# Value rows of a routed expert mixer gathered and summed one step behind the dot products, with the weights formed behind the next routing

## What is computed

```
q      = normalised h @ w_pq                   # 8 heads, two halves each
i_top  = top 16 of 128 keys in each half
e      = top 16 of the 16 x 16 sums            # 16 experts of 16384, per token and head
act    = gelu(h . expert_u[e])                 # 16 dot products of 1024
out    = sum over heads and 16 experts of softmax(score) * act * expert_v[e]
y      = layer_norm(alpha * h + out)
```

## Time and profile before

| | us |
|---|---|
| median of three runs | 4612.75 |
| the profiled execution's own time | 4595.0 |
| its span | 4593.3 |
| first dot product of step 0, from the span's start | 1032.9 |
| first gather, last gather's end | 1016.0, 4573.2 |
| mean granted TensorE clock | 0.745 |

### The profile page before, as it was taken

The page is one execution under the profiler, slowest core; times in us unless marked ns, Lnnn a source line. Parts: engine busy times, 40 slices in busy tenths (PEclk is TensorE's granted clock), DMA queues, the critical chain, the costliest instruction groups (busy, mean ns, idle before and its releaser), DMA issues.

```text
span 4593.3 us, 41900 instructions
## 1 busy us (share of the span) xinstructions
PE 2917.9 (64%) x12168; PEld 1561.3 (34%) x12168; DVE 2823.7 (61%) x6694; ACT 924.4 (20%) x2005; POOL 2398.5 (52%) x2288
## 2 busy tenths in 40 slices
PE   5877877877757567755565667776554555344343
PEld 3545555645314434422232234443122322011010
DVE  6577741244574366567776765656677667766764
ACT  1433110314311134411011123332110111000000
POOL 1010101213574465576775665656667667776776
PEclk8988988876678777767787776656777677676667
DMA  6476963436797787789999998877999899999998
GB/s 238 175 317 239 371 272 118 150 137 222 255 347 297 257 308 252 278 315 328 365 392 348 358 367 281 300 273 279 372 348 369 339 361 358 344 374 356 359 365 310
DMA packets 422338, 1388.96 MB, mean 302 GB/s; under 512 B 46374, under 2 KB 124454, under 8 KB 409822
## 3 DMA queue, kind: packets, MB, share of 16 engines
q0 software_dynamic: 306432, 1216.48, 71.1%
q1 hardware_dynamic: 89390, 140.65, 9.0%
q10 hardware_dynamic: 26288, 29.15, 1.8%
HBM read 1333.57 MB, written 56.86 MB: 303 GB/s over the span
## 4 chain that ended last, share of the span: by engine, by line
POOL 22%; PE 21%; issue 18%; DVE 6%; another core or an unknown queue 5%; DMA 5%; DVEq 2%; ACT 1%; ACTq 0%; SPq 0%; PEld 0%; PEldq 0%; POOLq 0%
POOL st_rows L1523 21%; PE st_ps_q L1786 3%; PE st_ps_m L1796 3%; PE st_ps_y L1870 3%; PE st_ps_q L1825 3%; DMA st_rows<-in_peer_u,st_expert 3%; PE st_ps_t L1769 2%; DMA st_rows<-in_peer_v,st_expert_v 2%; PE st_ps_m L1802 2%; PE st_ps_m L1738 1%; DVE st_rows L2103 1%; PE st_ps_s L1854 1%; DVEq L2116 1%; PE st_ps_q L1789 1%
## 5 line engine op out<-in xcount | busy, mean ns | idle before, releaser
L1523 POOL DMA_INDIRECT st_rows<-in_peer_v,st_expert_v x1024 | 1127.2, 1101 | 848.1 <-PE st_ps_y L1870 295.0
L2103 DVE CUSTOM_DVE_ANT_0 st_rows<-st_rows,st_h 128x1024 f32<-128x1024 f32 x1024 | 1233.2, 1223 | 366.5 <-DMA st_rows<-in_peer_u,st_expert 315.1
L1523 POOL DMA_INDIRECT st_rows<-in_peer_u,st_expert x1024 | 1135.9, 1109 | 535.0 <-issue 301.4
L1870 PE MATMUL st_ps_y<-st_rows,st_diag 128*32 128x512 f32 x4096 | 903.5, 725 | 291.7 <-DMA st_rows<-in_peer_v,st_expert_v 108.4
L1870 PEld LDWEIGHTS st_ps_y<-st_rows,st_diag 128*32 128x32 f32 x4096 | 189.6, 126 | 953.9 <-issue 450.9
L1854 PE MATMUL st_ps_s<-st_both,st_pick_tokens 128*128 128x32 f32 (+1 forms) x520 | 113.5, 379 | 602.1 <-DVEq L2149 340.5
L1825 PE MATMUL st_ps_q<-st_shared 128*128 128x128 f32 (+3 forms) x1024 | 273.7, 434 | 80.3 <-issue 78.9
L1854 PEld LDWEIGHTS st_ps_s<-st_both,st_pick_tokens 128*128 128x128 f32 x520 | 108.0, 306 | 635.2 <-issue 634.5
L602 PE MATMUL pd_ps<-pd_w,pd_xnT 128*128 128x256 f32 x1152 | 270.4, 394 | 25.8 <-ACT pd_stage L511 14.0
L2138 DVE TENSOR_TENSOR st_shared<-st_shared,st_ps_m 128x256 f32<-128x256 f32 (+5 forms) x176 | 73.5, 418 | 344.8 <-PE st_ps_m L1796 257.2
L1825 PEld LDWEIGHTS st_ps_q<-st_shared 128*128 128x128 f32 x1024 | 202.7, 222 | 155.6 <-issue 105.3
(11 more groups left out here) (326 smaller groups left out, 3921.6 us busy)
## 6 DMA issues: line engine op xcount, KB each, us to landing
st_shared<-in_w_pq_heads SPq DMA_DIRECT2D x32, 1024.0 KB
st_rows<-in_peer_u,st_expert POOLq DMA_INDIRECT x1024
st_rows<-in_peer_v,st_expert_v POOLq DMA_INDIRECT x1024
pd_w<-in_w_in SPq DMA_DIRECT2D x14, 1024.0 KB
scr_proj<-pd_stage ACTq DMA_DIRECT2D x8, 1152.0 KB
hs_step<-scr_factors SPq DMA_DIRECT2D x20, 416.0 KB
scr_score<-st_sc_out ACTq DMA_DIRECT2D x64, 130.0 KB
st_sc<-scr_score SPq DMA_DIRECT2D x64, 130.0 KB
```

The lines of the kernel that those rows point to most:

```text
L1523: pool.indirect_dma_start(rows[n % R][:, :], None, src, bass.IndirectOffsetOnAxis(ap=idx, axis=0)).then_inc(row_loaded[n % R], 16)
L1870: ins = nc.tensor.matmul(ps_y[j * QUAD:(j + 1) * QUAD, c * 512:(c + 1) * 512], diag[k % 2][:, QS * j + q, :], rows[n % R][:, c * 512:(c + ...
L2103: nc.vector.tensor_tensor_reduce(out=rows[n % R][:, :], in0=rows[n % R][:, :], in1=hb, scale=1.0, scalar=0.0, op0=ALU.mult, op1=ALU.add, a ...
```

## The change

Gathering and summing of the value rows move one step back against the dot products. POOL gathers u(0), u(1), v(0), u(2), v(1) and so on, and the ring's numbering follows. DVE runs best_keys(k+2) and route(k+2) right behind the dots of step k and only then `weights(k)`; `value_inputs(k-1)` moves into the dots of step k, behind the fourth one; so does `read_sums` at the second step of a block (the table `read_at`), and `second_norm` at that step's end. PE does `values(k-1)` and then `spread_both(k)`. The sample's gathers, dots and sums move one step later in the same way. No instruction of the arithmetic is added or dropped.

```diff
-    row_u = lambda k, s: (32 * k if k < SAMPLE_AFTER else 32 * k + 16) + s
-    row_v = lambda k, s: row_u(k, s) + K
+    row_u = lambda k, s: (32 * k - K if k > 0 else 0) + (2 * H if k > SAMPLE_AFTER else 0) + s
+    row_v = lambda k, s: (32 * k + 2 * K if k + 1 < STEPS else 32 * k + K) + (2 * H if k >= SAMPLE_AFTER else 0) + s
+    read_at = {H * b + H + 1: b for b in range(FB - 1) if H * (b + 1) != SAMPLE_AFTER}
+    read_at[SAMPLE_AFTER + 1] = SAMPLE_BLOCK
...
+            def gather_values(k):
+                pool.wait_ge(ev_ready, k + 1)
+                for s in range(K):
+                    c = QS * (s % QS) + s // QS
+                    gather(row_v(k, s), v_rows, expert_v[k % 4][:, c:c + 1])
...
             for k in range(STEPS):
                 pool.wait_ge(e_ready, k + 1)
                 for s in range(K):
                     gather(row_u(k, s), u_rows, expert[k % 4][:, s:s + 1])
-                pool.wait_ge(ev_ready, k + 1)
-                for s in range(K):
-                    c = QS * (s % QS) + s // QS
-                    gather(row_v(k, s), v_rows, expert_v[k % 4][:, c:c + 1])
+                if k > 0:
+                    gather_values(k - 1)
...
+            gather_values(STEPS - 1)
...
+                if k > 0:
+                    values(k - 1)
                 spread_both(k)
-                values(k)
...
+            values(STEPS - 1)
...
                     dot(row_u(k, s), h[b % 2][:, :], act_in[k % 2][:, s:s + 1])
+                    if s == 3:
+                        if k > 0:
+                            value_inputs(k - 1)
+                        if k in read_at:
+                            read_sums(k // H - 1 + (k > SAMPLE_AFTER), read_at[k])
...
                 dots(k)
-                if pending is not None:
-                    read_sums(finished, pending)
-                weights(k)
                 if k + 2 < STEPS:
                     best_keys(k + 2, 0)
-                value_inputs(k)
...
                 if k + 2 < STEPS:
                     route(k + 2)
+                weights(k)
```

More of the change, by code:

```diff
@@ L1466, in _ @@
                     load_tail(k - SAMPLE_ROUTE_STEP - 1)
-                if k == SAMPLE_AFTER:
+                if k == SAMPLE_AFTER + 1:
                     store_y(SAMPLE_AFTER // H - 1, SAMPLE_AFTER // H - 1)
+                elif k == SAMPLE_AFTER + 2:
                     store_y(SAMPLE_AFTER // H, SAMPLE_BLOCK)
-                elif k % H == 0 and k > 0:
-                    store_y(unit_no(k) // H - 1 + (k > SAMPLE_AFTER), k // H - 1)
+                elif k - 1 in read_at:
+                    store_y(read_at[k - 1], read_at[k - 1])
                 if k in MIX:
@@ L1524, in gather @@
                                         bass.IndirectOffsetOnAxis(ap=idx, axis=0)).then_inc(row_loaded[n % R], 16)
-            for k in range(STEPS):
+            def gather_values(k):
[3 more added lines that the diff above has]
+                    gather(row_v(k, s), v_rows, expert_v[k % 4][:, c:c + 1])
+            for k in range(STEPS):
+                pool.wait_ge(e_ready, k + 1)
+                for s in range(K):
+                    gather(row_u(k, s), u_rows, expert[k % 4][:, s:s + 1])
+                if k > 0:
+                    gather_values(k - 1)
                 if k == SAMPLE_AFTER:
@@ L1532, in _ @@
                         gather(row_sv(s), v_rows, te[:, s:s + 1])
-                pool.wait_ge(e_ready, k + 1)
-                for s in range(K):
-                    gather(row_u(k, s), u_rows, expert[k % 4][:, s:s + 1])
-                pool.wait_ge(ev_ready, k + 1)
-                for s in range(K):
-                    c = QS * (s % QS) + s // QS
-                    gather(row_v(k, s), v_rows, expert_v[k % 4][:, c:c + 1])
+            gather_values(STEPS - 1)
         @block.scalar
@@ L1701, in _ @@
                     act.drain().then_inc(exp_ready, 1)
-                if k == SAMPLE_AFTER - 1:
+                if k == SAMPLE_AFTER:
                     act.wait_ge(t_dots, 1)
@@ L1861, in values @@
                 if hd == 0 and k > 0:
-                    pe.wait_ge(y_read, unit_no(k) // H + (k > SAMPLE_AFTER))
+                    pe.wait_ge(y_read, k // H + (k >= SAMPLE_AFTER))
                 pe.wait_ge(diag_ready, k + 1)
@@ L2197, in _ @@
             route(1)
-            finished = 0
             for k in range(STEPS):
                 dots(k)
-                pending = None
-                if k == SAMPLE_AFTER:
-                    pending = SAMPLE_BLOCK
-                elif k % H == 0 and k > 0:
-                    pending = k // H - 1
-                if pending is not None:
-                    read_sums(finished, pending)
-                weights(k)
                 if k + 2 < STEPS:
                     best_keys(k + 2, 0)
-                value_inputs(k)
                 if k == 0:
@@ L2225, in _ @@
                     dve.drain().then_inc(te_ready, 1)
-                if pending is not None:
-                    second_norm(pending)
-                    finished += 1
+                if k in read_at:
+                    second_norm(read_at[k])
                 if k in SCALE:
@@ L2232, in _ @@
                     first_norm(MIX[k])
-                if k == SAMPLE_AFTER - 1:
+                if k == SAMPLE_AFTER:
+                    read_sums(SAMPLE_AFTER // H - 1, SAMPLE_AFTER // H - 1)
                     for s in range(H):
@@ L2242, in _ @@
                     dve.drain().then_inc(t_diag_ready, 1)
-                    read_sums(finished, SAMPLE_AFTER // H - 1)
                     second_norm(SAMPLE_AFTER // H - 1)
-                    finished += 1
-            read_sums(finished, FB - 1)
+            value_inputs(STEPS - 1)
+            read_sums(FB, FB - 1)
             second_norm(FB - 1)
```

5 lines of the change are left out of this document (2 added, 3 removed).

## The result

| | before | changed |
|---|---|---|
| median of the runs, us | 4607.22 (4580.68 to 4636.0, 4 runs) | 4456.73 (4437.55 to 4470.65, 4 runs) |
| profiled execution, its span | 4595.0, 4593.3 | 4437.55, 4435.8 |
| mean granted TensorE clock | 0.745 | 0.796 |

The account below looks back on a forecast made before the run. Attention steps were taken as bound by a chain of waits with DMA idle, plain steps by POOL's issuing (42.4 of 46.5 us). Terms summed to 203 us: 4595.0 to 4392, forecast 4400, range 4335 to 4490.

Parts of the forecast that it names:

- attention (19 steps): Steps 0 to 2, 8 to 14, 28 to 36: next dots begin about 6 us sooner in thirteen fully woven steps; -92 us.
- projection and norms (9): Steps 4, 5, 16 to 18, 38 to 41: the wait in value_inputs for `mix` leaves the path; -45 us, bounds 0 and -75.
- scores (16): Steps 20 to 27, 42 to 49: value_inputs out and weights last shorten the path behind ACT's copies; -30 us, bounds 0 and -55.
- four heads (6, 7): Steps 6 and 7, PE doing 46 to 70 us of scores in a row: DVE's diag no longer between; -6 us.
- sample (55 to 57): Sample rows, step 55, 72.8 us: the sample's own gathers, 21 us, stay; -10 us.
- plain steps (14): About 20 steps: POOL's 4 us tile wait goes, long gathers return 2 to 3; -1 us each, -20, bounds -4 and +8.
- tail from step 63: Start and end: first gather and the tail behind the last gather stay, the last being a value row in both; 0 us.
- the 12.1 us: Attention steps: the next step's rows arrive and its dots begin 12.1 us after the dots end, instead of 18.5.
- the start of the sums at -2: Attention steps: PE starts `values(k-1)` about 2 us before the dots end.
- rival 3: Dots phase of 43 non-attention steps: gap-free dots starve POOL's gathers, +5.3 us each, 4725 us; chance 0.05 for above 4640.
- the 8 us ascribed to `mix`: Step 16: DVE's 8.03 us wait in value_inputs, read as waiting for PE's `mix` ahead of `spread_both`.
- Rival 1: Transfers cap at 363 GB/s: plain and score steps keep their time, only steps with idle DMA gain; 4442 us, chance 0.12.

Follow-up runs that it names:

- quiet: Condition of the chip in the third and fourth comparisons, where the kernel before took 4159 and 4157 us; when stalled it took 4624 and 4636 us.
- fourth comparison: The changed kernel, unaltered, run once more beside the kernel before (4157 us): 4204.3 us, ratio 1.010 [1.008, 1.013].
- the kernel before with the gap: Kernel before, with a DVE drain behind each dot in steps 3, 15, 19, 37 and 50 to 63: 4174.5 us, ratio 1.0045 against the kernel before.
- first profile: Profiled execution of the changed kernel in its first measurement: 4437.55 us; the runs' median was 4456.73 us, ratio 0.967 to the kernel before.
- again, stalled: The changed kernel, no edit, run again beside the kernel before (4636 us): 4478.0 us, ratio 0.968 [0.962, 0.975].
- weights first: Changed kernel with `weights(k)` put back directly behind `dots(k)`, the values still lagging: 4475.7 us, ratio 0.983 to the kernel before.
- the stalled version with gaps everywhere: Changed kernel with a DVE drain behind every dot product, 1056 of them: 4486.1 us, ratio 0.983 to the kernel before.

## Why the prediction was right, and where it was not

Changes of stretches against the kernel before, us; the quiet column sets the fourth comparison's profile against that of the kernel before with the gap, on another chip. That kernel is itself 0.45% slow, and the two profiled executions were the slowest of the one kernel and the fastest of the other, so the column's sum is 20 us above the difference of the medians:

| term | forecast | first profile | again, stalled | quiet |
|---|---|---|---|---|
| attention (19 steps) | -92 | -122 | -82 | +7 |
| projection and norms (9) | -45 | -24 | -25 | -38 |
| scores (16) | -30 | -25 | -28 | +4 |
| four heads (6, 7) | -6 | -21 | -31 | 0 |
| sample (55 to 57) | -10 | -3 | +2 | +13 |
| plain steps (14) | -20 | +12 | +21 | +35 |
| start | 0 | +2 | -2 | +5 |
| tail from step 63 | 0 | +24 | +28 | +24 |
| sum | -203 | -157 | -117 | +50 |

**Attention, right.** The chain, the 12.1 us and the start of the sums at -2 were read off the trace and came out at 12.7 and -2.1; swapping PE's two calls took the gain away. The -92 lies between the two stalled profiles, whose granted clocks in steps 28 to 36 are 0.76 and 0.66. When quiet the same steps gain nothing: the slack that the chain showed was there only while the chip stalled.

**The tail, wrong.** The forecast said that start and end stay, since the last gather is a value row in both. It forgot that behind the last dots sixteen more value rows are still to be asked for. The rows were put off from steps 0 to 2, where POOL had time, to the end, where it has none; 24 to 28 us.

**Plain steps, wrong.** The forecast let POOL's wait for tiles, 4 us, go, took 2 to 3 us for long gathers, and -1 as the balance. The wait did not go: it moved from value row 13 to the second expert_u row of the next step, as above, and stayed at about 3 us; of POOL's time outside the gathers only 0.5 us a step went in the steps 58 to 62. In the quiet profiles, that of the kernel before with the gap and that of the changed kernel, there is no such wait, and nothing for the change to gain. The long gathers cost 3.0 us a step (180.28 - 165.46 over five steps), the upper end of the 2 to 3 forecast, and 3.7 when quiet (182.50 - 163.77). Together +2.5 us a step in 58 to 62, 3.8 quiet: inside the bounds of -4 to +8, but on the other side of zero. The forecast's own sign for that, plain steps above 47 us with gathers of 1.9 us in the dots phase, came true at 48.6 us. This is rival 3's mechanism, at 2.5 to 3.8 us a step rather than 5.3 net, in the plain steps and not in the other 29 of its 43. The forecast also counted about 20 plain steps; beside the steps of its other terms there are 16, the 14 of the table and 56 and 57, which the table has with the sample.

**Projection and norms, half of it.** Of the 8 us ascribed to `mix`, 5.9 were PE's delay behind it, and weights first did as well. **Scores, about right** while stalled, though for the lag and not, as the forecast's second half had it, for the weights' place.

**The sum, partly luck.** The change was worth 117 to 157 us of the 203 forecast, by the profiles. The plain steps had the wrong sign, the tail was missing, attention gave more than its share in the profile with the high clock, and the range reached far enough to hold the rest. That the chip was stalled in the deciding comparison was no part of the forecast.

**Rival 1 when quiet.** Near 366 GB/s and share 0.97 the attention steps have nothing to fill, as that rival said of steps with 363 GB/s. The cap is POOL's issuing and the transfers together: the quiet steps 42 to 49 moved 400 GB/s over 363 us. The Trainium skill (HBM Reference, section "Specifications (TRN2)") gives about 358 GB/s per core as effective. The same section has that figure as a core's share while both cores of a domain stream, and about 425 GB/s for a core that streams alone. The rows of one core at work, 366 to 400 GB/s, lie between the two, so the 47 us that the forecast worked out from 358 is no bound here.

The 0.05 for slower was too small for what the trace could have told: rows with "remote" and waits without a releaser carried part of the slack, and I priced that slack as the kernel's own.

## What to carry to other kernels

Before filling a slack, ask of each wait whether its releaser's own row ends when the wait ends; slack made of stops that the trace cannot name may be gone in the next run, and then only the price of the change is left (-3.3% became +1.0%). A software lag moves its first step's work to the end: it is free only if the end has room. And work put among paced operations makes them run in bursts; ask which engine needed the gaps.

## What was not expected of the hardware

- A gap of 0.22 us between VectorE's dots, a drain each, shortens GpSimd's indirect gathers from 1.99 to 1.06 us. With its 0.30 us of issue a gather is two dot periods of 1.15 us in the one case and one of 1.37 in the other. The Trainium skill (SBUF — State Buffer, section "SBUF: two separate sides") tells of an exclusive lock on a port pair that the two engines share; these figures agree with it.
- The same kernel on the same chip took 4636 and 4157 us, 10% apart. The changed kernel's quiet and stalled profiles moved the same 1389 MB, and in the stalled ones PE's semaphore updates come up to some 10 us behind the ends of its rows, in the quiet ones never over 0.5.
- A score projection takes 7.4 us in every quiet profile and 12 to 28 in the stalled version with gaps everywhere, where PE had stood 5.5 to 7.2 us before each. The granted clock fell there, but five of the eight second halves ran at 1.00 and still took 6.6 to 8.0 us, where 3.6 is the quiet figure. Faster gathers upstream cost 34 us in that stretch.
